# Channel fold by reflection: GpSimd forms the sums and differences of mirrored channels ahead of the fold's matmuls

## The chip, the cores and the metric

The kernel runs on all 8 cores of one Trainium2 chip. Each core computes one of the 8 sequences of the batch, and every core does the same work on its own data with its own copy of the weights. The metric is the device time of the slowest core in microseconds (us). The engines are called PE (TensorE), DVE (VectorE), ACT (ScalarE), POOL (GpSimd) and SP (SyncE, which only issues transfers here). POOL also issues transfers, and those of its transfers that read float32 and write bf16 convert on the way; they are called casts below where they go from memory to memory.

## The reference

Two layers, each with a norm, a token mixer, a gate and a residual. The change lies in the first layer's mixer, a two-dimensional Fourier transform over the 4096 positions and over the 256 channels of each of 8 groups, of which the real part is kept:

```python
def fourier_mixer(h, w_in, w_out):
    b, s, _ = h.shape
    proj = h @ w_in                                  # (s, 1024) @ (1024, 4096)
    xin, z = proj[..., :D_INNER], proj[..., D_INNER:]
    xg = xin.reshape(b, s, N_GROUPS, GROUP_DIM).astype(jnp.float32)   # 8 groups of 256
    y = jnp.fft.fft2(xg, axes=(1, 3), norm="ortho").real
    y = y.astype(h.dtype).reshape(b, s, D_INNER)
    return (y * jax.nn.silu(z)) @ w_out
```

The second layer is a gated mixer over chunks of 128 positions (`sgu_mixer`); the change does not touch it.

## The kernel before

The transform over channels is not applied to the 4096 rows of activations but to the weights: for each group g, `fold(g)` multiplies the 256 rows of the branch weight (bf16, two tiles `wb` of 128 channels x 1024) with a table `fmat` of 256 channels x 256 columns: 128 cosines and 128 sines, with the cosine of harmonic 128 in the place of the sine of harmonic 0. The result `wp[g % 2]` (1024 x 256, bf16) is then the weight of the group.

The layer runs through these stages, one after the other on PE:

- The first loop, over 32 tiles `s` of 128 rows: load (`load_x`, SP), square (ACT), `norm` (two small POOL instructions, then DVE), eight transposes into `hT` (PE, DVE), a first transform step `U` (PE), which is stored to `Ud` (SP), and in between gate projections `zgroup(hb, zt)`: eight matmuls of 512 columns, a SiLU by ACT into the tile `sz[zt % 6]`. `zt` is one of 16 blocks of gate channels with its weight `wz[zt % 6]`; `hb` is one of 8 blocks of 512 rows.
- The position transform, `qd` from 7 down to 0: PE reads `V` (loaded from `Ud` by 32 transfers on SP) and writes `H` through ACT and DVE. `fold(0)` is spread over qd 4 to 1.
- The group loop, g from 0 to 7: `pq(g)` (128 matmuls of 260 columns on `H` and `wp[g % 2]`, then DVE forms sum and difference), `gate(g)` (DVE multiplies the result into `sz[2g % 6]` and `sz[(2g+1) % 6]`, and puts a store of each of these two tiles to `gyT` on a list), then `fold(g+1)`, then the gate projections `zall(zt)` of two further blocks: 6, 7 after pq(1), 8, 9 after pq(2), 10, 11 after pq(3), 12 to 15 after pq(4). The block zt writes the tile that block zt - 6 had, so its first SiLU waits until that tile's store to `gyT` has landed.
- The passage to the second half: the stored `gyT` is read back as `gyt`, and the output projection `out0` starts.

Four things order the work around the change. Each engine, and each queue of transfers, works through its instructions in program order; a wait holds up all that stands behind it. `tick()` is called after each `qd` of `pq` and each `zgroup` of `zall`; every fourth call issues one cast of the later layers' weights (32 casts of 512 KB written, on POOL, `precasts`), and every fourth call also takes one store off the list (SP). A cast waits for the eighth one before it (`d_pc[n % 8]`). And PSUM has six float32 banks in turn (`next_f`), so PE can be six banks ahead of ACT.

Before, `wb` is loaded by POOL with conversion, two tiles per group, into slots of which two lie under `wp[1]` and four under `V`. The lines of the profile that matter are L431 (the fold's matmuls), L269 (its copy to `wp`), L412 and L416 (matmul and SiLU of a `zgroup`), L595 (`pq`), L626 (the gate's multiplies), L399 and L401 (the norm's POOL instructions), L166 (every transfer) and L114 (every wait of a queue).

## Time and profile before

| | us |
|---|---|
| median of three runs | 1583.35 |
| lowest of them | 1580.53 |
| the profiled execution | 1582.04 |
| its span on the slowest core, core 1 | 1580.7 |
| spans of all eight cores | 1564.3 to 1580.7 |

| engine, core 1 | busy us | share |
|---|---|---|
| PE | 1545.7 | 98% |
| DVE | 747.1 | 47% |
| ACT | 515.9 | 33% |
| POOL | 156.4 | 10% |

The profile follows one execution on its slowest core. Times of rows are microseconds from the start of the span; the span leaves 1.3 us of that execution's own time outside. A busy PE is not a PE at its peak, since matmuls overlap; the spacing of their starts is what one costs in a sequence.

### The profile page before, as it was taken

Reading aid. Unit: us, or ns where it says so; the run is one execution under the profiler, and the core shown is the slowest. Engines: PE = TensorE matmul, PEld = TensorE weight load, DVE = VectorE, ACT = ScalarE, POOL = GpSimd, SP = SyncE. Lnnn points to the kernel's source line nnn. Section 1 sums busy time; section 2 is a strip of 40 time slices with the busy share of each in tenths; the row PEclk is TensorE's granted clock in tenths of the full one; section 3 lists DMA queues with packets and bytes.
Section 4 is the critical chain, followed back from the end, with each engine's and each line's share of the span. In section 5 each row is a group of like instructions: output and inputs, shape, how many; then the busy total and the mean of one; then the engine's idle time right before and its main releaser. Section 6 shows DMA issues by size and latency. Waiting matters only on the chain.

```text
span 1580.7 us, 25439 instructions; the slowest of 8 cores (1564.3 to 1580.7 us)
## 1 busy us (share of the span) xinstructions
PE 1545.7 (98%) x8458; PEld 782.7 (50%) x8458; DVE 747.1 (47%) x1245; ACT 515.9 (33%) x915; POOL 156.4 (10%) x336
## 2 busy tenths in 40 slices
PE   6999999999899999999999999999999999999997
PEld 3557766646644444544444444445444444544443
DVE  5866532213636435624553463356245435624552
ACT  5766333333223313322331232133123313322331
POOL 3311111010211011001000100110010011001000
PEclk9999999999999999999999999999999999999999
DMA  9986999999887941643453155335324531643411
GB/s 256 288 249 170 171 139 152 152 144 180 250 205 189 242 176 48 226 150 98 152 199 125 38 188 199 107 116 201 134 69 167 207 113 47 226 152 96 148 46 54
DMA packets 103298, 247.72 MB, mean 157 GB/s; under 512 B 40042, under 2 KB 56042, under 8 KB 87402
## 3 DMA queue, kind: packets, MB, share of 16 engines
q1 hardware_dynamic: 53652, 207.76, 39.8%
q0 software_dynamic: 15568, 29.63, 14.9%
q10 hardware_dynamic: 33952, 8.72, 3.3%
q8 instruction: 71, 1.16, 0.3%
q14 instruction: 55, 0.45, 0.1%
HBM read 225.24 MB, written 58.87 MB: 180 GB/s over the span
## 4 chain that ended last, share of the span: by engine, by line
PE 94%; DMA 4%; DVE 1%; issue 1%; ACT 0%; SPq 0%; POOL 0%; DVEq 0%; ACTq 0%; POOLq 0%
PE pf L848 28%; PE pf L751 27%; PE pf L412 14%; PE pf L821 14%; PE pf L595 5%; PE pf L858 2%; DMA gy<-sz_77 1%; DMA a0x_59<-xt 1%; DMA gyt<-gy 1%; PE pb L481 1%; PE pf L491 1%; PE pf L558 1%; DMA h1T<-xn_0_2525 1%; PE pf L431 1%; SPq L166 0%
## 5 line engine op out<-in xcount | busy, mean ns | idle before, releaser
L751 PE MATMUL pf<-W_2513,gyt 128*128 128x512 bf16 x992 | 219.2, 382 | 7.4 <-DMA gyt<-gy 7.4
L751 PE MATMUL pf<-W_2524,u 128*128 128x512 bf16 x1024 | 222.3, 379 | 0.0
L751 PEld LDWEIGHTS pf<-W_2513,gyt 128*128 128x128 bf16 x992 | 97.6, 98 | 126.6 <-issue 13.0
L751 PEld LDWEIGHTS pf<-W_2524,u 128*128 128x128 bf16 x1024 | 100.2, 98 | 120.8
L851 ACT ACTIVATE u<-pf 128x512 bf16<-128x512 f32 x128 | 76.5, 597 | 164.2 <-PE pf L848 154.7
L825 ACT ACTIVATE v<-pf 128x512 f32<-128x512 f32 x128 | 75.4, 597 | 121.1 <-PE pf L821 101.6
L848 PE MATMUL pf<-h1T,ring_2522 128*128 128x512 bf16 x416 | 96.8, 385 | 0.0
L848 PE MATMUL pf<-h1T,ring_2519 128*128 128x512 bf16 x416 | 96.5, 382 | 0.0
L848 PE MATMUL pf<-h1T,ring_2523 128*128 128x512 bf16 x416 | 95.5, 380 | 0.0
L848 PE MATMUL pf<-h1T,ring_2520 128*128 128x512 bf16 x416 | 94.9, 379 | 0.0
L848 PE MATMUL pf<-h1T,ring_2521 128*128 128x512 bf16 x384 | 88.3, 379 | 0.0
L605 DVE TENSOR_TENSOR Dt_93<-pc_97,pf 128x256 bf16<-128x256 f32 x28 | 11.8, 421 | 144.9 <-PE pf L595 120.8
L862 DVE SCALAR_TENSOR_TENSOR ytmp_2532<-pf,gTs,TT 128x512 f32<-128x512 f32 x64 | 48.1, 751 | 48.6 <-PE pf L858 48.5
L742 POOL TENSOR_SCALAR sm_2546<-sm_2546 128x1 f32<-128x1 f32 x24 | 5.3, 221 | 631.6 <-ACT sqj L787 588.0
L848 PEld LDWEIGHTS pf<-h1T,ring_2522 128*128 128x128 bf16 x416 | 40.1, 99 | 44.4 <-issue 5.2
L848 PEld LDWEIGHTS pf<-h1T,ring_2523 128*128 128x128 bf16 x416 | 39.8, 98 | 43.8 <-issue 1.5
L848 PEld LDWEIGHTS pf<-h1T,ring_2519 128*128 128x128 bf16 x416 | 39.8, 98 | 43.6 <-issue 3.5
L848 PEld LDWEIGHTS pf<-h1T,ring_2520 128*128 128x128 bf16 x416 | 39.6, 98 | 43.3 <-issue 0.3
L851 ACT ACTIVATE sg_2543<-pf 128x512 bf16<-128x512 f32 x64 | 38.2, 598 | 69.2 <-PE pf L848 58.9
L851 ACT ACTIVATE sg_2544<-pf 128x512 bf16<-128x512 f32 x64 | 38.2, 598 | 67.6 <-PE pf L848 64.4
L595 PE MATMUL pf<-H,wp_85 128*128 128x260 bf16 x512 | 58.3, 276 | 0.0
L595 PE MATMUL pf<-H,wp_84 128*128 128x260 bf16 x512 | 57.6, 274 | 0.0
(298 smaller groups left out, 2317.8 us busy)
## 6 DMA issues: line engine op xcount, KB each, us to landing
ring_2519<-wind SPq DMA_DIRECT2D x20, 1024.0 KB, 7.4
ring_2520<-wind SPq DMA_DIRECT2D x19, 1024.0 KB, 7.1
ring_2521<-wind SPq DMA_DIRECT2D x19, 1024.0 KB, 6.7
ring_2522<-wind SPq DMA_DIRECT2D x19, 1024.0 KB, 7.1
ring_2523<-wind SPq DMA_DIRECT2D x19, 1024.0 KB, 6.4
gyt<-gy SPq DMA_DIRECT2D x7, 2048.0 KB, 12.4
wind<-w_in1p POOLq DMA_DIRECT2D x24, 512.0 KB, 42.1
V<-ud SPq DMA_DIRECT2D x32, 256.0 KB, 7.9
```

Source lines behind the costliest of these rows:

```text
L412: pe.op(lambda e: e.matmul(bank[:], w[:, dc, :], hT[:, dc, hb * 512:(hb + 1) * 512], start=(dc == 0), stop=(dc == 7)), [wb_, hTb[hb], hTal ...
L431: pe.op(lambda e: e.matmul(bank[:, h * 256:(h + 1) * 256], wb[wb_slot(2 * g + kc)][0][:, dc * 128:(dc + 1) * 128], fmat[:, kc, :], start=( ...
L481: pe.op(lambda e: e.transpose(out=bank[:, dc * 128:(dc + 1) * 128], in_=xn_[:, dc * 128:(dc + 1) * 128], identity=ident[:]), [xnb, identb] ...
L491: pe.op(lambda e: e.matmul(bank[:], tr[:], xn_[:, h * 512:(h + 1) * 512], start=True, stop=True), [trb, xnb], [bb], waw=False)
L595: pe.op(lambda e: e.matmul(bank[:, 0:HQ], w_[:, dc, cs * 128:(cs + 1) * 128], H[:, qd, dc, cs, :], start=(dc == 0), stop=(dc == 7)), [wpb, ...
L751: pe.op(lambda e: e.matmul(bank[:], lhs(kc), rhs[:, kc, nh * 512:(nh + 1) * 512], start=(kc == 0), stop=(kc == 15)), lb(kc) + rb(kc), [bb] ...
L821: pe.op(lambda e: e.matmul(bank[:], h1T[:, dc, t * 128:(t + 1) * 128], r_[:, dc, :], start=(dc == 0), stop=(dc == 7)), [h1Tb[t], rb], [bb] ...
L825: act.op(lambda e: e.activation(out=vj, in_=bank[:], func=AF.Gelu_apprx_tanh), [bb], [vjb])
L848: pe.op(lambda e: e.matmul(bank[:], r_[:, dc, c0:c0 + 128], h1T[:, dc, :], start=(dc == 0), stop=(dc == 7)), h1Tb + [rb], [bb], waw=False, ...
L851: act.op(lambda e: e.activation(out=out_ap, in_=bank[:], func=func), [bb], wb_)
L858: pe.op(lambda e: e.matmul(bank[:, t * 128:(t + 1) * 128], vhat[t][0][:, ct * 128:(ct + 1) * 128], wsT[:, ct // 2, :], start=True, stop=True),
L862: dve.op(lambda e: e.scalar_tensor_tensor(out=y_[:].rearrange("c (t p) -> c t p", p=128), in0=bank[:].rearrange("c (t p) -> c t p", p=128) ...
```

## The change

The cosines of channel c and channel 256 - c are equal, and their sines are opposite. So the fold needs only the sum of the two channels' weights for the cosines and the difference for the sines: 128 channels instead of 256 in each.

- The weights come as `wbE`, pairs of channels (c, 256 - c) in float32, in eight groups of four quarters of 256 columns. SP loads one quarter (128 x 2 x 256 float32, 256 KB) into a single staging tile `st`, and two POOL instructions write its sum and its difference as bf16 into `eo[:, 0]` and `eo[:, 1]`. `sums()` is a generator that does this in program order: one call issues the load, the next the two POOL instructions. Channels 0 and 128 make up the first pair; the even harmonics take its sum and the odd ones its difference, and so the harmonics are sorted even first (`_HARM`).
- `fold` takes one matmul of 129 columns on the sums and one of 192 on the differences in place of two of 256.
- The calls: one per tile in tiles 10 to 17 of the first loop (group 0), two after each of qd 7 to 4 (group 1), then one per `tick` (group 2 in pq(0), group 3 in pq(1), group 4 in zall(6); from group 4 on a group starts only when the fold two groups before it has been issued, so groups 5, 6, 7 come in zall(8), zall(10), zall(12)). `fold(g)` first issues what is missing.
- `eo` has four places: under `wp[1]`, under `wz[0]` and `wz[1]`, and two under `V`. As group 1 lies on `wz[0]` and `wz[1]`, the loads of the gate weights 6 and 7 move from the end of the position transform to after fold(1).
- The loads of `wb` on POOL are gone.

```diff
-            wb = [tile(f"wb{i}", [128, D], BF16, ...) for i in range(6)]
+            eo = [tile(f"eo{i}", [128, 2, D], BF16, o) for i, o in enumerate((top["at"] - 4096, wzo, vh, vh + 4096))]
...
+            st, stb = tile("st", [128, 2, 256], F32, top["at"] - 2048)
...
-            def load_wb(i):
-                k = wb_slot(i)
-                pool.dma(wb[k][0][:], wb_in[i], d_wb[k], writes=[wb[k][1]])
+            def eo_of(g):
+                return eo[g if g < 2 else 2 + g % 2]
+
+            folded = {"n": 0, "summed": 0}
+
+            def sums():
+                for g in range(8):
+                    eo_, eob = eo_of(g)
+                    while g > 3 and folded["n"] < g - 1:
+                        yield
+                    for q in range(4):
+                        sp.dma(st[:], wb_in[g, q], d_st, writes=[stb], waw=True)
+                        yield
+                        for k, op in enumerate((ALU.add, ALU.subtract)):
+                            pool.op(lambda e: e.tensor_tensor(out=eo_[:, k, q * 256:(q + 1) * 256], in0=st[:, 0, :],
+                                                              in1=st[:, 1, :], op=op), [stb], [eob], waw=False)
+                        folded["summed"] += 1
+                        yield
...
             def fold(g, dcs):
+                while folded["summed"] < 4 * g + 4:
+                    next(summing)
...
-                        for kc in range(2):
-                            pe.op(lambda e: e.matmul(bank[:, h * 256:(h + 1) * 256],
-                                                     wb[...][0][:, dc * 128:(dc + 1) * 128], fmat[:, kc, :],
+                        for k, f, a, z in ((0, fE, 0, 129), (1, fO, 64, 256)):
+                            pe.op(lambda e: e.matmul(bank[:, h * 256 + a:h * 256 + z], eo_[:, k, dc * 128:(dc + 1) * 128], f,
+                                                     start=(k == 0), stop=True, skip_group_check=(k == 1)),
...
-                    if 0 < g < 6:
-                        load_wb(2 * g + 4)
-                        load_wb(2 * g + 5)
+                    folded["n"] = g + 1
...
-                if s in (12, 14):
-                    load_wb(s // 2 - 6)
+                if 10 <= s < 18:
+                    next(summing)
...
                 if ticks["n"] % 4 == 1:
                     next(casts, None)
+                next(summing, None)
                 if stores and ticks["n"] % 4 == 0:
                     stores.pop(0)()
...
+                if folded["summed"] < 8:
+                    next(summing)
+                    next(summing)
                 if qd == 0:
-                    load_wb(2)
-                    load_wb(3)
-                    for i in range(6, 9):
-                        load_wz(i)
-                    load_wb(4)
-                    load_wb(5)
-                    for i in range(9, 11):
+                    for i in range(8, 11):
                         load_wz(i)
...
                     fold(1, range(4))
                     for hb in range(6, 8):
                         zgroup(hb, 5)
-                    load_wz(11)
+                    for i in (6, 7, 11):
+                        load_wz(i)
```

## Rows read from the trace of the kernel before

**Rows 1.** The page's chain that ended last: shares by engine and by line.

```profile
PE 94%; DMA 4%; DVE 1%; issue 1%; ACT 0%; SPq 0%; POOL 0%; DVEq 0%; ACTq 0%; POOLq 0%
```

**Rows 2.** Waits of PE: who was waited for, total us, times, longest.

```profile
PE pf L751 <- DMA gyt<-gy: 7.4, 1, 7.4
```

**Rows 3.** Chain at the passage, in order of time: start, us, what.

```profile
387.37 0.42 DVE Dt_93 L605
...
394.63 18.68 DMA gy<-sz_77
...
428.92 14.62 PE pf L751 x58
```

**Rows 4.** Chain in the group loop, a fold and a pq: start, us, what.

```profile
164.94 1.75 PE pf L431 x16
...
214.77 14.19 PE pf L595 x128
```

**Rows 5.** Timeline of PE, qd 4: start, us, instruction.

```profile
130.89 1.06 PE L558 MATMUL pf<-bdt,V 128*128 128x128 bf16 x16
131.78 0.27 PE L431 MATMUL pf<-cpk,wb_86 128*128 128x256 bf16 x1
```

**Rows 6.** POOL's groups by form: count, busy us, mean ns, idle before.

```profile
L626 POOL TENSOR_TENSOR szsp<-p_100,szsp 8x224 bf16<-8x224 f32 x1 | 0.6, 614 | 0.1
L626 POOL TENSOR_TENSOR szsp<-p_100,szsp 8x32 bf16<-8x32 f32 x1 | 0.3, 330 | 0.1
```

**Rows 7.** Timeline of POOL in the first loop: start, us, instruction, idle before.

```profile
59.57 0.22 POOL L399 TENSOR_SCALAR stats<-stats 128x1 f32<-128x1 f32 x1 [1.60 <-ACT a0xn_61 L391]
```

**Rows 8.** Timeline of SP's queue: start, us to issue, transfer.

```profile
107.51 20.81 SPq L166 DMA_DIRECT2D V<-ud  x32
169.25 0.33 SPq L166 DMA_DIRECT2D gy<-sz_72  x1
172.35 0.33 SPq L166 DMA_DIRECT2D gy<-sz_73  x1
...
381.20 0.34 SPq L166 DMA_DIRECT2D szsp<-zrow  x1
```

**Rows 9.** Transfers by line, several stretches: count, KB each, us to landing.

```profile
V<-ud SPq DMA_DIRECT2D x32, 256.0 KB, 7.9
out<-x_1_2516 SPq DMA_DIRECT2D x1, 256.0 KB, 2.1
gy<-sz_72 SPq DMA_DIRECT2D x1, 1024.0 KB, 16.7
gy<-sz_73 SPq DMA_DIRECT2D x1, 1024.0 KB, 20.0
gy<-sz_76 SPq DMA_DIRECT2D x1, 1024.0 KB, 13.0
wb_88<-wbT POOLq DMA_DIRECT2D x1, 256.0 KB, 5.4
zrow<-sz_75 ACTq DMA_DIRECT2D x3, 8.0 KB
```

**Rows 10.** Timeline of ACT, gate blocks 15 and 6: start, us, instruction.

```profile
373.85 0.20 ACTq L166 DMA_DIRECT2D zrow<-sz_75  x1
...
189.02 0.60 ACT L416 ACTIVATE sz_72<-pf 128x512 bf16<-128x512 f32 x1 [0.36 <-PE pf L412]
```

**Rows 11.** Timeline of PE, gate blocks 6 and 7.

```profile
186.98 13.98 PE L412 MATMUL pf<-hT,wz_78 128*128 128x512 bf16 x64
200.79 13.98 PE L412 MATMUL pf<-hT,wz_79 128*128 128x512 bf16 x64
```

**Rows 12.** One stretch: busy us of PE, PEld, DVE, ACT, POOL; clock, DMA share, GB/s.

```profile
187.00:215.00 28.00, 28.00 (x134) 12.84 (x132) 5.06 (x8) 10.57 (x21) 4.44 (x7) 1.00 1.04 180
```

**Rows 13.** Stretches around PE's wait at the passage, same columns.

```profile
427.00:429.00 2.00, 0.08 (x1) 0.11 (x2) 1.69 (x4) 0.00 (x0) 0.00 (x0) 0.50 0.97 314
431.00:433.00 2.00, 2.00 (x7) 0.78 (x6) 0.00 (x0) 0.00 (x0) 0.00 (x0) 0.59 0.90 287
```

47 lines of the change are left out of this document (25 added, 22 removed).

## The prediction

> **What bounds the kernel now.** I read the chain that ended last first: PE holds 94% of it [rows 1], so only what shortens or stalls PE's sequence moves the end. The waits of PE come next. In the whole group loop there is no wait worth the name; the one large wait is 7.4 us at the passage to the output projection, for the read-back of `gy` [rows 2]. Then the chain around that passage, in order of time: it leaves PE at the end of pq(5), goes over DVE's gate from 387.4, then over the store of `sz_77` issued at 394.6 and the read-back, and returns to PE at 428.9 [rows 3]. So PE time saved before 387 reaches the end; PE time saved between 387 and 421 only lengthens the 7.4 us wait. Last the stretches: from 187 to 215, gate blocks 6 and 7, the transfer engines are full (share 1.04) while they move only 180 GB/s [rows 12]; the casts fill them. The reader should keep that in mind: the change touches PE a little and the queues a lot.
>
> **The fold's matmuls.** Sixteen matmuls of 256 columns take 1.75 us, 109.4 ns each [rows 4]. Sixteen of 128 columns with a new weight each start at 130.89 and the next instruction at 131.78, so 55.6 ns each [rows 5]. Between the two points a column costs 0.42 ns: 129 columns 56 ns, 192 columns 82.5 ns. A pair falls from 218.8 to 138.5 ns, 80 ns saved; 8 pairs per fold save 0.64 us, 8 folds 5.1 us. Folds 6 and 7 lie behind pq(5), in the stretch that only feeds the 7.4 us wait. Folds 0 to 5 count: **-3.85 us**. The bounds are 0 (weight loads or ACT's copies set the pace) and -5.1.
>
> The Trainium skill speaks against part of this: TensorE: Matmul & The Clock Gate, section Back-to-back issue gap, gives about 81 ns for a sustained weight load and matmul of 128 columns and 131 ns for 512. An estimate from that page puts the pair at about 170 ns, the saving at 0.39 us a fold, and the sum 1.5 us later. This case's trace disagrees at 128 columns, with 55.6 ns [rows 5], and the row decides.
>
> **The sums on POOL.** No row has 128x256 float32. The nearest two-input row is 8x224 with 614 ns, and 8x32 took 330 ns: 1.48 ns an element, so 0.66 us at 256 and 1.3 us for the pair [rows 6]. Bounds: 0.66 (the two overlap entirely) and 2 us. In all 32 pairs, 42 us of an engine that is 10% busy. In the first loop a pair stands between two norms, where POOL idles 1.60 us per tile [rows 7]; 1.3 us fit, so I take 0, with a bound of 4 pairs x (2.0 - 1.6) = 1.6 us lost.
>
> **The loads, moved from POOL's queue to SP's.** There is one staging tile, so a quarter is a cycle: transfer, pair of sums, next transfer. Alone, 256 KB landed 2.1 us after its issue [rows 9]; with the sums I take a cycle of 4.1 us (transfer 2.8). Among the casts no load of this size was on SP. The lower bound is that same 2.1 us, the upper 13.0 us, the quickest gate store of 1 MB [rows 9]. The nearest row is an 8 KB transfer issued by ACT at 373.85, for which SP waited until 381.20: 7.4 us for hardly any data [rows 8 to 10]. Two gate stores issued 3.1 us apart landed after 16.7 and 20.0 us, so the second came 6.4 us behind the first [rows 8, 9]; a quarter of that would put 256 KB at 9.0. I take 8.5 us, and 9.8 us for a cycle. The bytes read are the same as before, and the `wb` loads' share of the queue is given back, so I price the total traffic at 0; its bound is 5 us either way at the passage, where the casts' end decides how long the 8 KB transfer takes.
>
> **Where this meets the path.** SP works in order. A store of a gate tile now stands behind a quarter whose transfer may not be issued before the last pair of sums, and POOL's casts and `wz` loads stand behind the sums. I follow the order through groups 1 to 4.
>
> - Group 1: the 32 V transfers are issued by 128.3, the last lands 7.9 us later [rows 8, 9], at 136. With nothing else moving, four cycles of 4.1 end at about 150.5. POOL then issues wz 8 to 10 and three casts.
> - Group 2: the first quarter lands before the casts fill the engines, sums done at 155.3. Three cycles of 9.8 would give 184.7; the casts issued by then run out towards 178, so I take 182. Only now come the loads of wz 6 and 7. The quickest load of that kind landed in 5.4 us [rows 9]: 188. PE reaches gate block 6 at 186.98 less three folds, 185.1 [rows 11]. **Stall 3 us** (0 to 6).
> - Group 3: after three `wz` loads and a cast, the first pair is done at about 190. Behind it SP issues the store of `sz_72`, at 190.4 where it was 169.25 [rows 8]. With the quickest 13 us [rows 9] it lands at 203. The first SiLU of block 6 writes that tile; before, it ran at 189.02, 3 us after the store had landed (169.25 + 16.7) [rows 8 to 10]. Six banks of 1.73 us (13.81 us for eight [rows 11]) let PE go on from 188 to 198.4. **Stall 5 us** (2 to 7).
> - The store of `sz_73` comes after the third quarter, which itself queues behind the store of `sz_72`: issued at about 206 where it was 172.35, landed at 218. Block 7 starts on PE at 207 and can run to 217.4. **Stall 1.5 us** (0 to 6).
> - Group 4: `sz_74` and `sz_75` land at about 235 and 250; blocks 8 and 9 start at about 237 and 251 and have 10.4 us of banks: none. Groups 5 to 7 begin one per 43 us of PE and a group takes some 35 us: none.
>
> The sum of the stalls is **+9.5 us**, between 4 and 15. A pause of PE has a further price: at the passage, where PE had paused for 7.4 us [rows 2], the granted clock was 0.50, the lower level of 1.2 GHz, at 427 to 429 and still 0.59 on average in 431 to 433, when PE worked again [rows 13]. Some 4 us at half speed lose 2 us; for a pause of 5 us I take that as the upper bound and leave it in the range. Against the execution's own time: 1582.0 - 3.85 + 9.5 = 1587.7, so **1588**; the median of the three runs shown is 1.3 us above that execution.
>
> **Rivals.**
>
> - **The waits stay hidden; the saving alone.** If a quarter among the casts takes 4 us rather than 8.5, group 2 ends at about 169, wz 6 is there in time, the store of `sz_72` leaves at 175 and that of `sz_73` at 194, and the six banks cover both. For it speaks that POOL, held by the sums, has fewer casts in flight than before; against it the 7.4 us for 8 KB [rows 8 to 10]. 1582.0 - 3.85 = 1578, or 1582 if the shorter matmuls save nothing.
> - **The cycle is longer, 10 to 12 us.** Then wz 6 lands at 191 or later, the stalls are about 6, 8 and 5, fold(2) waits for its sums as well, and the clock falls in each pause: 1600 (1598 to 1615).
> - **The slower side: the cycle passes PE's period.** PE spends about 43.6 us on a group: pq 14.2 and fold 1.75 [rows 4], two gate blocks 27.6 (13.81 each [rows 11]). With two stores queued between, a group of four quarters takes 2 x 9.8 + 2 x 14.3 = 48 us if each store holds its quarter for its full 13 us. Should that hold in every group, the lag is carried on: the store of `sz_74` in block 12 leaves some 25 us after block 14 wants the tile, and folds 6 and 7 wait too. It decides from 43.6 us a group on, that is from a cycle of about 8 us beside fully serial stores. Price 30 to 45 us: 1612 to 1625. Against it speaks that a POOL that waits issues no casts, so that the queue drains and the cycle shortens by itself.
> - **Faster by over 2%** would need 32 us. All folds together are 8 x 1.75 = 14 us, and the passage holds 7.4 more; I see no way.
>
> **How the numbers follow.** Forecast (1588, its own range 1580 to 1598) 0.46; saving alone 0.30; longer cycle 0.13; the carried lag 0.09; faster by over 2% 0.02. The range from 1574 to 1606 holds the first two cases, the first with the passage's 5 us either way, and more than half of the third. Two per cent, 32 us, is about what a measurement of this kernel can tell from no change. Within it lie the first three cases, 0.89; slower 0.09; faster 0.02.
>
> **What would show it.** In the profile after: `fold` at about 1.1 us where it was 1.75; POOL pairs of 1.3 us, no norm in the first loop delayed by more than 1 us; quarters that land in 2 to 3 us before 150 and in 8 to 9 after; PE waits at blocks 6 and 7, the first on the load of wz 6, the next through ACT's SiLU on the stores of `sz_72` and `sz_73`, 4 to 15 us in all; stores at about 190 and 206. If PE has no wait between 180 and 220, the saving-alone case holds. If PE waits again in block 9 or later, or a fold waits on sums after group 3, it is the carried lag. A stall in the first loop would be something that I have priced at nothing.

## The result, and the profile after

| | before | after |
|---|---|---|
| executions without a disturbance, us | 1580.53, 1583.08, 1583.35 | 1591.96, 1592.44 |
| ratio after to before, 95% interval | | 1.0062 [1.0033, 1.0092] |
| span of the slowest core in the profiled execution, us | 1580.7 (core 1) | 1590.6 (core 4) |

The changed kernel is 9.9 us later, 0.6%. Two of its four executions were disturbed on one die (1654.83 and 1881.68) and are left out, as is one of the kernel before. The page and the rows below are of core 4. In the changed kernel L454 is the fold, L432 and L436 the matmul and the SiLU of a `zgroup`, L614 is `pq`, L770 `out0`, L399 the sums, L419 and L421 the norm on POOL, L172 every transfer.

The chain that ended last, shares by engine, now holds a term that it did not have [rows 1]: PE's part fell from 94% to 89%, and transfers rose from 4% to 7%. A line further down on the page gives the quarters `st<-wbE` 3% of the span.

```profile
PE 89%; DMA 7%; POOL 1%; DVE 1%; issue 1%; ACT 0%; DVEq 0%; ACTq 0%; POOLq 0%; SPq 0%
```

Waits of PE (engine, line, releaser: us in all, times, longest). The first answers to [rows 2]. The `a0xn_60` one is the start of the program and was 8.2 us before as well (core 6).

```profile
PE pf L770 <- DMA gyt<-gy: 9.2, 1, 9.2
PE pb L502 <- DVE a0xn_60 L423: 8.1, 1, 8.1
PE pb L502 <- DVE hT L505: 5.4, 4, 2.9
PE pf L454 <- POOL eo_88 L399: 4.9, 1, 4.9
PE pf L432 <- DMA wz_78<-wz: 3.8, 1, 3.8
```

PE's timeline around the first of the moved loads (start, us, instructions, idle before and its releaser). It answers to [rows 11]: block 6 started at 186.98 and took 13.98 us; it now starts at 198.90 and takes 16.51, and the fold before it waits too.

```profile
192.77 2.30 PE L454 MATMUL pf<-cpk,eo_88 128*128 128x129 bf16 x16 [4.93 <-POOL eo_88 L399]
198.90 16.51 PE L432 MATMUL pf<-hT,wz_78 128*128 128x512 bf16 x64 [3.83 <-DMA wz_78<-wz]
215.24 7.07 PE L432 MATMUL pf<-hT,wz_79 128*128 128x512 bf16 x32
```

The stretches of that place (busy us of PE, PEld, DVE, ACT, POOL; granted clock, DMA share, GB/s), the third as in [rows 12]. The clock falls to the lower level of 1.2 GHz once PE has paused, is still there in 199 to 201, when PE works without a gap, and is back at 2.4 GHz in 205 to 207. The transfer engines, full in this stretch before (1.04), are at 0.73, and at 0.22 in 150 to 160 (0.90 before, on core 1).

```profile
193.00:196.00 3.00, 2.07 (x16) 1.69 (x13) 2.46 (x4) 2.35 (x5) 1.82 (x4) 0.50 0.31 81
199.00:201.00 2.00, 2.00 (x6) 0.63 (x6) 0.00 (x0) 0.00 (x0) 0.00 (x0) 0.50 1.03 83
187.00:215.00 28.00, 19.25 (x87) 9.29 (x86) 7.27 (x13) 6.60 (x14) 9.77 (x15) 0.76 0.73 143
150.00:160.00 10.00, 8.84 (x82) 6.91 (x82) 4.99 (x16) 5.16 (x14) 4.63 (x8) 1.00 0.22 55
205.00:207.00 2.00, 2.00 (x11) 0.88 (x9) 0.00 (x0) 0.00 (x0) 0.00 (x0) 1.00 1.06 356
```

The chain of waits through group 2, and a later fold. Load, sums, load, sums: one staging tile, and quarters that land in 10 us. The fold of 1.13 us answers to the 1.75 of [rows 4].

```profile
163.97 10.12 DMA st<-wbE
...
174.22 2.31 POOL eo_88 L399 x2
...
176.59 9.80 DMA st<-wbE
...
192.46 6.03 DMA wz_78<-wz
...
243.41 1.13 PE pf L454 x16
```

The two gate stores on SP's queue, where [rows 8] has 169.25 and 172.35, and the SiLUs of ACT that wait for them.

```profile
198.95 0.63 SPq L172 DMA_DIRECT2D gy<-sz_72  x1
...
214.31 1.08 SPq L172 DMA_DIRECT2D gy<-sz_73  x1
```

```profile
210.96 3.54 ACT L436 ACTIVATE sz_72<-pf 128x512 bf16<-128x512 f32 x7 [14.54 <-DMA gy<-sz_72]
...
221.06 1.08 ACT L436 ACTIVATE sz_73<-pf 128x512 bf16<-128x512 f32 x2 [4.96 <-DMA gy<-sz_73]
```

POOL's timeline, first at the end of group 0 in the first loop, then at groups 6 and 7. Three things are to be seen. At 72.89 a pair waits 3.31 us for its quarter, and the norm of a tile stands behind it. From 326 to 372 POOL mostly waits for quarters, as long as 10.84 us for one. And the casts, which one tick in four should issue one by one, go out five and six together as soon as a group's last pair is done; the last six, and the load of `wsT` that stands behind all casts, leave at 368 to 372. In the kernel before, POOL ran ahead and issued `wsT` at 345.0 on the slowest core.

```profile
64.13 1.86 POOL L399 TENSOR_TENSOR eo_86<-st 128x256 bf16<-128x256 f32 x2
...
72.89 1.41 POOL L399 TENSOR_TENSOR eo_86<-st 128x256 bf16<-128x256 f32 x2 [3.31 <-DMA st<-wbE]
74.39 0.22 POOL L419 TENSOR_SCALAR stats<-stats 128x1 f32<-128x1 f32 x1
...
327.41 3.41 POOL L172 DMA_DIRECT2D wind<-w_in1p  x5
332.83 1.49 POOL L399 TENSOR_TENSOR eo_89<-st 128x256 bf16<-128x256 f32 x2 [2.02 <-DMA st<-wbE]
345.15 1.41 POOL L399 TENSOR_TENSOR eo_89<-st 128x256 bf16<-128x256 f32 x2 [10.84 <-DMA st<-wbE]
...
357.47 1.40 POOL L399 TENSOR_TENSOR eo_89<-st 128x256 bf16<-128x256 f32 x2 [10.25 <-DMA st<-wbE]
367.00 1.41 POOL L399 TENSOR_TENSOR eo_89<-st 128x256 bf16<-128x256 f32 x2 [8.14 <-DMA st<-wbE]
368.36 4.07 POOL L172 DMA_DIRECT2D wind<-w_in1p  x6
372.40 0.59 POOL L172 DMA_DIRECT2D wsT<-w_sT  x1
```

The wait at 72.89 reaches PE. DVE's scaling behind that norm waits 3.32 us, then PE's transposes wait 2.93, and the eight matmuls of a `zgroup` behind them take 2.92 us where the eight just before the pause took 1.89. The last of these rows is the stretch in which that happens, with a granted clock of 0.53, mostly the lower level of 1.2 GHz. On core 4 this is nearly all of the 4.8 us that the first loop loses: 2.93 of waiting, and some 1.6 at the lower clock (an estimate: 3.40 us at 0.53).

```profile
77.59 0.87 PE L502 MATMUL pb<-ident,a0xn_61 128*128 128x128 bf16 x8 [2.93 <-DVE hT L505]
...
79.11 2.92 PE L432 MATMUL pf<-hT,wz_78 128*128 128x512 bf16 x8
...
77.60:81.00 3.40, 3.40 (x15) 1.72 (x16) 3.40 (x5) 0.60 (x1) 0.22 (x1) 0.53 1.00 200
```

The same comparison by stage, from the starts on PE's timelines of every core in the two profiled executions (range over the eight cores, us):

| stage | before | after |
|---|---|---|
| end of the first loop | 99.2 to 101.8 | 104.1 to 109.0 |
| pq(0) to pq(1), one fold | 19.4 to 19.6 | 18.8 |
| pq(1) to pq(2), one fold, blocks 6 and 7 | 43.6 to 44.6 | 47.4 to 55.6 |
| pq(2) to pq(3), one fold, blocks 8 and 9 | 43.6 | 42.9 |
| pq(4) to pq(5), one fold, blocks 12 to 15 | 71.2 | 70.6 |
| start of `out0` | 419.8 to 428.9 | 432.4 to 443.2 |
| start of `out0` to the end | 1144 to 1154 | 1145 to 1148 |

Core 4 of both: the first loop gives +4.8, five folds give -0.64 each, pq(1) to pq(2) gives +12.7 beside its fold's -0.64, and pq(7) to `out0` +0.9; `out0` starts 15.1 us later. From the slowest core of before to the slowest of after it starts 14.3 us later (428.9 on core 1, 443.2 on core 4). Nearly all of that is PE's lateness at the end of pq(5): the chain at the passage begins on DVE at 399.96 where it began at 387.37 [rows 3], 12.6 us later, and from there to `out0` it takes 43.2 us where it took 41.6.

```profile
399.96 0.42 DVE Dt_91 L624
...
407.22 20.87 DMA gy<-sz_77
...
431.73 11.09 DMA gyt<-gy
...
443.17 14.28 PE pf L770 x58
```

Of the 14.3 us only 9.9 arrive, since core 1 before took 1151.8 us from `out0` to the end and core 4 after takes 1147.4. The rows for this lie in the kernel before. Behind the passage its core 1 has five stretches, 27.5 us in all, with a granted clock of 0.81, between the two levels of 1.2 and 2.4 GHz, while PE is busy throughout; two of them are shown. They cost some 5.2 us (an estimate: 0.19 of 27.5). Cores 0, 2 and 3 have such stretches too; cores 4 to 7 have none, and no core of the changed kernel has any.

```profile
442.80:449.00 6.20, 6.20 (x25) 2.61 (x24) 2.10 (x3) 1.15 (x2) 0.79 (x2) 0.81 0.97 383
...
955.30:961.90 6.60, 6.60 (x27) 2.72 (x25) 2.00 (x5) 1.79 (x3) 0.00 (x0) 0.81 0.76 286
```

Among cores 4 to 7 alone the slowest takes 1574.6 us before (core 6) and 1590.6 after, 16.0 us or 1.0% more. So 9.9 us is what was measured, and the change by itself probably costs more. Whether the timed executions of the kernel before had such stretches is not on record.

### The profile page after: what moved, and what is told of

Same layout as the page of the kernel before. It is cut to its first block, busy times and chain, and to the rows that moved or that the text cites. A ratio compares the mean times of both kernels' runs of the same rounds, so it can differ in the third digit from the quotient of the medians.

```text
span 1590.6 us, 25582 instructions; the slowest of 8 cores (1578.3 to 1590.6 us)
## 1 busy us (share of the span) xinstructions
PE 1539.8 (97%) x8458; PEld 779.0 (49%) x8458; DVE 750.2 (47%) x1245; ACT 514.6 (32%) x915; POOL 195.9 (12%) x384
## 3 DMA queue, kind: packets, MB, share of 16 engines
q0 software_dynamic: 13264, 25.43, 12.6%
## 4 chain that ended last, share of the span: by engine, by line
PE 89%; DMA 7%; POOL 1%; DVE 1%; issue 1%; ACT 0%; DVEq 0%; ACTq 0%; POOLq 0%; SPq 0%
PE pf L867 28%; PE pf L770 27%; PE pf L840 14%; PE pf L432 13%; PE pf L614 4%; DMA st<-wbE 3%; PE pf L877 2%; DMA gy<-sz_77 1%; DMA a0x_54<-xt 1%; DMA gyt<-gy 1%; PE pb L502 1%; DMA h1T<-xn_0_2559 1%; PE pf L512 1%; PE pf L580 0%; DMA wz_78<-wz 0%
## 5 line engine op out<-in xcount | busy, mean ns | idle before, releaser
L770 PE MATMUL pf<-W_2547,gyt 128*128 128x512 bf16 x992 | 218.1, 381 | 9.2 <-DMA gyt<-gy 9.2
L770 PE MATMUL pf<-W_2558,u 128*128 128x512 bf16 x1024 | 222.3, 379 | 0.0
L770 PEld LDWEIGHTS pf<-W_2547,gyt 128*128 128x128 bf16 x992 | 97.3, 98 | 127.5 <-issue 11.6
L770 PEld LDWEIGHTS pf<-W_2558,u 128*128 128x128 bf16 x1024 | 100.2, 98 | 120.8
L881 DVE SCALAR_TENSOR_TENSOR ytmp_2566<-pf,gTs,TT 128x512 f32<-128x512 f32 x64 | 48.1, 751 | 48.8 <-PE pf L877 48.5
L867 PEld LDWEIGHTS pf<-h1T,ring_2556 128*128 128x128 bf16 x416 | 39.7, 98 | 43.2
L867 PEld LDWEIGHTS pf<-h1T,ring_2554 128*128 128x128 bf16 x416 | 39.6, 98 | 43.2
L614 PE MATMUL pf<-H,wp_84 128*128 128x260 bf16 x512 | 57.6, 274 | 1.0 <-ACT wp_84 L462 1.0
L614 PE MATMUL pf<-H,wp_85 128*128 128x260 bf16 x512 | 57.4, 274 | 0.0
```

The costliest lines, as they stand in the source:

```text
L614: pe.op(lambda e: e.matmul(bank[:, 0:HQ], w_[:, dc, cs * 128:(cs + 1) * 128], H[:, qd, dc, cs, :], start=(dc == 0), stop=(dc == 7)), [wpb, ...
L770: pe.op(lambda e: e.matmul(bank[:], lhs(kc), rhs[:, kc, nh * 512:(nh + 1) * 512], start=(kc == 0), stop=(kc == 15)), lb(kc) + rb(kc), [bb] ...
L867: pe.op(lambda e: e.matmul(bank[:], r_[:, dc, c0:c0 + 128], h1T[:, dc, :], start=(dc == 0), stop=(dc == 7)), h1Tb + [rb], [bb], waw=False, ...
L881: dve.op(lambda e: e.scalar_tensor_tensor(out=y_[:].rearrange("c (t p) -> c t p", p=128), in0=bank[:].rearrange("c (t p) -> c t p", p=128) ...
```

## The experiments

Each ratio is to runs of the kernel before on the same chip. The three groups of four kernels ran on three chips; on these the kernel before had medians of 1575.34, 1574.12 and 1574.15 us. The changed kernel itself did not run beside these runs. Its 1.0062 (1.0033 to 1.0092) comes from executions beside which the kernel before took some 8 us longer than it takes here, so the ratios below can't be set against it closely. Run 12, less the 3.2 us that five shorter folds save, gives an estimate of 1.0075 for it on the third chip, if that saving reaches the end.

**1. The short matmuls alone.**

The base is the kernel before.

```diff
-                        for kc in range(2):
-                            pe.op(lambda e: e.matmul(bank[:, h * 256:(h + 1) * 256],
-                                                     wb[wb_slot(2 * g + kc)][0][:, dc * 128:(dc + 1) * 128], fmat[:, kc, :],
+                        for kc, a, z in ((0, 0, 129), (1, 64, 256)):
+                            pe.op(lambda e: e.matmul(bank[:, h * 256 + a:h * 256 + z],
+                                                     wb[wb_slot(2 * g + kc)][0][:, dc * 128:(dc + 1) * 128], fmat[:, kc, a:z],
```

> The kernel before, loads and all, but the fold takes one matmul of 129 and one of 192 columns from its two weight tiles in place of two of 256. It leaves out part of the fold's sum, so only its time is of use. It measures the saving alone. By spacings of rows of before (55.6 ns at 128 columns, 109.4 at 256): a fold of 1.11 us where it was 1.75, 0.64 us saved per fold, 3.85 us on the path; ratio to before 0.9976. By the page TensorE: Matmul & The Clock Gate of the Trainium skill, section Back-to-back issue gap (81 ns at 128 columns), an estimate of 0.39 us a fold and 0.9985. If ACT's copies set the pace of a fold, nothing: 1.000.

Measured: 1.0013 [1.0003, 1.0022]. Every fold is 0.64 us shorter: pq(1) to pq(2) takes 42.9 us on all eight cores. The gain is nevertheless gone at the end. Four cores (1, 2, 4, 6) end after 1557.0 to 1563.5 us, the other four after 1569.9 to 1573.3; the first start `out0` at 413 to 418, the second at 424 to 427. On core 5, a late one, PE waits for the read-back longer than in [rows 2]; core 1, an early one, has no such wait:

```profile
PE pf L751 <- DMA gyt<-gy: 11.6, 1, 11.6
```

So the first term of the prediction is right on PE and is given back at the passage, on the cores that end last. I took from this a second theory: from 150 on the transfer engines are a bound of their own. The rows of the kernel before fit it; in every stretch of 10 us from 160 to 370 and on every core the DMA share is 0.93 or more.

**2. Group 0's sums later in the first loop.** The base of this run and of the next four is the changed kernel.

```diff
-                if 10 <= s < 18:
+                if 22 <= s < 30:
                     next(summing)
```

> The changed kernel, with group 0's loads and sums in tiles 22 to 29 of the first loop, where no more x tiles are loaded, in place of tiles 10 to 17. First theory: the first loop lost its 3 to 8 us because a pair of sums waited on POOL for its quarter behind x tiles on SP's queue, with the next norm behind it. Then the loop ends at 99 to 102 us on every core as before (it ended at 104 to 109), and the time falls by 3 to 6 us, ratio to before about 1.003. Rival: the pairs of sums themselves, 1.9 us each between norms that leave 1.6 us, cost it: 4 x 0.3 us and no more is recovered by moving them, the loop ends at 104 or later, ratio unchanged at 1.006.

Measured: 1.0074 [1.0061, 1.0087]. The loop ends at 102.4 to 106.7: little is won. A pair takes less there (1.43 where it was 1.86), but waits for its quarter as before, on core 2 of this run:

```profile
87.44 1.43 POOL L399 TENSOR_TENSOR eo<-st 128x256 bf16<-128x256 f32 x2 [2.08 <-DMA st<-wbE]
...
94.70 1.42 POOL L399 TENSOR_TENSOR eo<-st 128x256 bf16<-128x256 f32 x2 [3.40 <-DMA st<-wbE]
```

**3. Three staging tiles for group 2** (two in the place of group 3's sums, which is free then).

```diff
+            st_ab = [tile(f"st_ab{i}", [128, 2, 256], F32, vh + 4096 + 2048 * i) for i in range(2)]
...
+                    if g == 2:
+                        places = [(st, stb), st_ab[0], st_ab[1], (st, stb)]
...
+                        for q in range(3):
+                            load(q)
+                        yield
+                        for q in range(4):
+                            sum_quarter(g, q, *places[q])
+                            if q == 0:
+                                load(3)
+                            yield
```

> The changed kernel, with three staging tiles for group 2 (two of them in the place that group 3's sums get later), so that three quarters are issued before the casts pile up. First theory, the serial cycle through one staging tile: group 2's sums end at about 168 in place of 192, fold(2) waits for nothing (it waited 4.9 us on core 4), PE's wait for the weight of block 6 goes (3.8 us), the store of sz_72 leaves at 176 to 180 in place of 199; from pq(1) to pq(2) PE takes 44 to 46 us where it took 47 to 56; the time falls by 4 to 8 us, ratio about 1.002. Rival: the transfer engines are simply full from 160 on, and the order of the quarters makes no difference: pq(1) to pq(2) stays above 47 us, ratio 1.006.

Measured: 1.0066 [1.0053, 1.0080]. fold(2) no longer waits, and pq(1) to pq(2) takes 42.9 to 49.0 us where it took 47.4 to 55.6. What is left there, on core 1, is the load of wz 6 behind the sums (3.4 us), and the store of `sz_72`, still at 191.39 behind a quarter of group 3. The serial cycle was thus one cause of the wait. `out0` starts at 418.3 to 432.3, 11 to 14 us before that of the changed kernel; how much of this arrives at the end the ratio can't tell, since the changed kernel did not run beside it.

**4. Runs 2 and 3 together, and group 3's sums not before block 6,** so that both gate stores go first.

```diff
-                next(summing, None)
+                if not 8 < ticks["n"] <= 16:
+                    next(summing, None)
```

> Both of these, and group 3's sums moved from pq(1) to gate block 6 (group 4's to block 7), so that the stores of sz_72 and sz_73 are not behind quarters in SP's queue. If the three losses (first loop, group 2's cycle, late stores) are all that the change adds, what is left is the saving of the shorter matmuls: no wait of PE over 1 us between the first loop and the passage, ratio 0.997 to 1.000. Rival: the stores come late again one pair of blocks further on, since group 3 and 4 now stand there: PE waits in blocks 8 and 9, ratio 1.001 to 1.005.

Measured: 1.0090 [1.0074, 1.0105], above both expectations, and later than run 3 on the same chip. On core 6 the stores leave from 173.45 on, close to [rows 8], and no SiLU waits for them; but the load of wz 6, issued at 176.5 with 2 MB of stores and seven casts around it, lands when PE has waited 14.4 us. pq(1) to pq(2) takes 49.4 to 60.2.

```profile
PE pf L459 <- DMA wz<-wz: 14.4, 1, 14.4
```

**5. No casts beside the quarters of groups 2 and 3.**

```diff
-                if ticks["n"] % 4 == 1:
+                if ticks["n"] > 16 and ticks["n"] % 4 == 1:
+                    next(casts, None)
+                if 16 < ticks["n"] <= 40 and ticks["n"] % 4 == 3:
                     next(casts, None)
...
-                    for _ in range(2):
-                        next(casts, None)
```

> The changed kernel without any cast before the 17th tick (pq(0) and pq(1) run without them); from there two per four ticks until the 40th, so that from the 40th tick on as many are issued as before. Theory (the quarters are late because they share the transfer engines with the casts, and the stores behind them are late for that): a quarter lands in 3 to 4 us, group 2 is summed by 165, wz 6 is loaded by 175, the stretch from pq(1) to pq(2) is 43 us on every core where it was 47 to 56, and the ratio is 1.000 to 1.003 (the first loop's 3 to 8 us stay). Rival (one staging tile and the order of the queues suffice for the stalls, whatever else is in flight): 48 to 55 us and 1.005 to 1.007.

Measured: 1.0153 [1.0137, 1.0169]. Both halves of this are of use. The theory's first half holds exactly: pq(1) to pq(2) is 42.9 to 43.0 us on all eight cores, every stall is gone. The ratio lies some 13 us above the higher of the two expectations. The time comes back later: pq(4) to pq(5) takes 75 to 83 us instead of 70.6, and `out0` starts at 440.7 to 452.7. On core 6 the transfer engines were half idle from 150 to 200 (0.51) and full afterwards:

```profile
150.00:200.00 50.00, 49.76 (x376) 35.97 (x377) 29.50 (x84) 18.08 (x41) 19.48 (x26) 0.97 0.51 122
...
300.00:380.00 80.00, 70.87 (x395) 38.20 (x394) 13.43 (x40) 21.24 (x43) 20.35 (x28) 0.97 0.96 157
```

and the gate stores of blocks 12 to 15 land late behind the casts that were put off (ACT waits 32.5 us for three of them between 300 and 385).

**6. Group 0 through four staging tiles** in the place of `sz5`, which the first loop does not use; `first_load(q)` loads quarter q into tile q, `first_sum(q)` issues its pair.

```diff
-                if 10 <= s < 18:
-                    next(summing)
+                if 8 <= s < 12:
+                    first_load(s - 8)
+                if s in (14, 17, 20, 23):
+                    first_sum((s - 14) // 3)
```

> The changed kernel with group 0 through four staging tiles of its own, in the place of sz5, which the first loop does not use: the loads are issued in tiles 8 to 11, the sums in tiles 14, 17, 20 and 23, so POOL never waits for a quarter there. Theory (the first loop loses its time because POOL waits for a late quarter and the norm stands behind it): the loop ends at 100 to 102 where it ended at 104 to 109, ratio 1.003 to 1.005. Rival (the pair of sums itself, 1.9 us there, delays the norm): the loop ends at 103 to 106 as in the run with the sums in tiles 22 to 29, ratio 1.006 to 1.007.

Measured: 1.0056 [1.0038, 1.0074]. The loop ends at 99.8 to 102.4, as in the kernel before. The pair still takes 1.86 us, but no longer waits:

```profile
59.98 1.86 POOL L411 TENSOR_TENSOR eo<-st 128x256 bf16<-128x256 f32 x2
...
69.99 1.86 POOL L411 TENSOR_TENSOR eo<-st 128x256 bf16<-128x256 f32 x2
```

This settles the first loop: it was the wait for a late quarter, with the norm behind it, and not the sums. The ratio lies 0.0019 below the estimate for the changed kernel, with an interval that reaches 0.0018 to either side.

**7. Denser casts from the 33rd tick on,** in the kernel of run 1.

```diff
-                if ticks["n"] % 4 == 1:
+                if (ticks["n"] % 4 if ticks["n"] <= 32 else ticks["n"] % 3) == 1:
```

> The kernel before with the short matmuls on the old tiles (the fold leaves out a part of its sum), as in the first of these runs, and from the 33rd tick on a cast every third tick in place of every fourth, so that the last is issued at about 325 where it was 370. Theory (the 3.85 us of the fold are given back at the passage, since the casts and the loads behind them fill the transfer engines from 300 to 410 at a rate of their own): the passage from pq(7) to the output projection takes 27 to 29 us on all cores where it took 27 to 38, and the ratio is 0.994 to 0.998. Rival 1 (the bytes of the passage alone set its end): unchanged, 1.000 to 1.002. Rival 2 (denser casts delay the gate stores of blocks 8 to 13): PE waits between 230 and 330, above 1.003.

Measured: 1.0020 [1.0009, 1.0032]. The edit did not do what it was for: `wsT`, behind the last cast, is issued at 336 to 352 as in run 1 (326 to 352). POOL waits 93.8 us for earlier casts, since a cast waits for the eighth before it. The casts go at the pace of the transfer engines, not of the ticks. It tells nothing more of the passage.

**8. Group 0 as in run 6, no cast before the 17th tick, then one every second tick.**

```diff
-                if ticks["n"] % 4 == 1:
+                if ticks["n"] > 16 and ticks["n"] % 2 == 1:
```

> The changed kernel with both: group 0 through the four staging tiles, and no cast before the 17th tick, from there one every second tick (the last is issued at about 290). If the losses are the late quarter in the first loop, the casts beside the quarters of groups 2 and 3, and the casts at the passage, the ratio is 0.994 to 0.999. If any of the three is something else, its size stays: 1.002 to 1.006. If the denser casts delay the stores of blocks 8 to 12, PE waits between 200 and 290 and the ratio is above 1.003 too.

Measured: 1.0210 [1.0156, 1.0264], from executions of 1602.3, 1602.4 and 1616.3 us. The first loop (100.0 to 101.6) and pq(1) to pq(2) (42.9) are whole, and pq(4) to pq(5) takes 105 to 110 us: the last named case, at a later place than named. On core 1, between 300 and 400, ACT's waits are

```profile
ACT sz L447 <- DMA gy<-sz: 54.9, 3, 22.5
```

Runs 5 and 8 have this in common: from 150 to 200 the transfer engines are about half used (0.51, and 0.55 on core 1 of run 8), and the casts that were put off go out more densely afterwards, beside the gate stores of blocks 12 to 15, which come late. Whether the unused time or the denser casts make the stores late these two runs do not part.

**9. The kernel before, with two casts moved into the gap of its transfers.** `pool.deps([Vb[0]], [])` lets POOL wait until the last V transfer has landed.

```diff
+            pool.deps([Vb[0]], [])
+            for _ in range(2):
+                next(casts)
             act.load = dve.load = 0.0
             for qd in range(7, -1, -1):
```

> The kernel before, whole, with one thing moved: its first two casts are issued as soon as the last V transfer has landed (about 137), in the stretch to 150 in which the transfer engines of the kernel before are empty; the others keep their ticks, so that each of them comes eight ticks, some 14 us, earlier. Theory (from 150 to 400 the transfer engines are a second bound beside PE, full in every stretch of 10 us, and their end sets the passage): about 13 us of transfer work move ahead, the loads behind the casts end earlier, the store of sz_77 lands in 12 to 15 us where it took 18.7, and PE's wait of 7.4 for the read-back shrinks to 0 to 3: ratio 0.994 to 0.998. Rival (what is transferred beside the passage does not set its end; PE and the gate do): 0.999 to 1.001.

Measured: 0.9987 [0.9978, 0.9997], 1572.1 us beside 1574.15. The gap was there (DMA share 0.01 from 137 to 150 before on core 1, 0.58 here on core 0), and PE's wait at the passage falls as expected, on core 6 to

```profile
PE pf L754 <- DMA gyt<-gy: 1.9, 1, 1.9
```

`out0` starts at 416.6 to 421.6 on all cores. The time falls by 2 us only, where 3 to 9 were expected. The interval reaches the theory's range at one end and the rival's (0.999 to 1.001) at the other, so it is the shorter wait, and not the time, that speaks for the theory. The spans still differ by 9 us from core to core (1560.3 to 1569.2), though `out0` starts within 5. On the slowest, core 0, PE waits once more behind the passage, for the load of `h1T`, and the granted clock is 0.50 from 452.6 to 456.0; core 1, which is early, has neither this wait nor one at the passage.

```profile
PE pf L824 <- DMA h1T<-xn: 2.9, 1, 2.9
```

This is the fastest whole kernel of the study, faster than both kernels of the case.

**10. The same two casts, with the short matmuls** (the edits of runs 1 and 9).

> The same two early casts in the kernel with the short matmuls on the old tiles (the fold leaves out a part of its sum). That kernel without the early casts had 1.0013: its 3.85 us were given back at the passage. Theory of the full transfer engines: with their work moved ahead the saving arrives, 0.0015 to 0.0025 below the run with the early casts alone: 0.992 to 0.996. Rival (the saving is lost in another place, or the passage is bound by PE and the gate): no lower than the run beside it, 0.998 to 1.001.

Measured: 0.9973 [0.9961, 0.9985]. That lies between the two ranges. Without the early casts these matmuls had 1.0013 [1.0003, 1.0022]: the interval is clear of it. The intervals of this run and of run 9 overlap, but both ran on the same chip, so that their times can be compared directly: five executions of 1568.8 to 1570.8 us here, ten of 1570.4 to 1573.6 us there, and the means differ by 2.3 us. That is some two thirds of what five folds save (3.2 us): most of the saving arrives once the transfers leave room for it.

**11. Other places and another order in the changed kernel.**

```diff
-                return eo[g if g < 2 else 2 + g % 2]
+                return eo[0 if g == 0 else 3 - g % 2]
...
+                    while g > 2 and ticks["n"] < 16:
+                        yield
...
-                    for i in range(8, 11):
+                    for i in range(6, 11):
                         load_wz(i)
```

> The changed kernel with other places and another order, and the same arithmetic: group 0 through the four staging tiles in the place of sz5; group 1's sums lie under V (as those of groups 3, 5, 7), through three staging tiles of which two lie where group 2's sums go, so that wz 6 and 7 are free and are loaded where they were before; group 3's sums start at the 17th tick, behind the stores of sz_72 and sz_73. Theory (the 4 to 13 us of the group loop are the displaced loads of wz 6 and 7 and the stores behind quarters): the first loop ends at 100 to 102, pq(1) to pq(2) takes 43 to 47, ratio 1.000 to 1.003. Rival (any sum that stands beside the casts holds the queues, wherever it lies): 48 or more there, or as much lost later, ratio 1.005 to 1.008.

Measured: 1.0119 [1.0100, 1.0138]. The first loop ends at 99.3 to 102.5 and pq(1) to pq(2) takes 42.9 to 48.2, at most 44.3 on seven cores: the theory of the stalls holds. But the ratio lies above both expectations. A part is lost before pq(0), which starts 50.5 to 54.3 us after the end of the first loop, where it was 48.8 in the kernel before; the larger part is lost at the passage. PE's wait there on core 3, the slowest:

```profile
PE pf L808 <- DMA gyt<-gy: 16.9, 1, 16.9
```

On this core pq(5) starts at 377.1, 8.4 us before core 4 of the changed kernel, and `out0` at 442.5, only 0.7 us before it. POOL's timeline ends alike in both: the quarters of group 7 one by one, then six casts at once.

```profile
356.70 1.41 POOL L426 TENSOR_TENSOR eo<-st 128x256 bf16<-128x256 f32 x2 [9.29 <-DMA st<-wbE]
367.67 1.41 POOL L426 TENSOR_TENSOR eo<-st 128x256 bf16<-128x256 f32 x2 [9.56 <-DMA st<-wbE]
369.01 4.06 POOL L172 DMA_DIRECT2D wind<-w_in1p  x6
373.06 0.58 POOL L172 DMA_DIRECT2D wsT<-w_sT  x1
```

**12. The staging alone: the changed kernel with long matmuls.**

```diff
-                        for k, f, a, z in ((0, fE, 0, 129), (1, fO, 64, 256)):
+                        for k, f in ((0, cpk[:, 0:256]), (1, cpk[:, 130:386])):
```

> The changed kernel with its fold made long again: two matmuls of 256 columns on the staged sums (the columns are not the reference's, so the fold computes another transform). This is the staging alone, without the saving. If the saving of 0.64 us per fold reaches the end in the changed kernel, this run is later than the changed kernel by 2.5 to 4 us: 1.0080 to 1.0095. If the transfer engines set the end there too, as in the run with the short matmuls on the old tiles, it stays at 1.0055 to 1.0070.

Measured: 1.0095 [1.0081, 1.0110]. It lies in the range of the first case, and the changed kernel's 1.0062 below it; but that was not measured beside it, and its interval goes up to 1.0092. That the saving reaches the end in the changed kernel is likely by this and not shown.

**One view over all of them.** When POOL has issued its last cast it issues the load of `wsT`. From there to the first matmul of `out0`, over all eight cores of each profiled execution:

| kernel | `wsT` issued, us | `out0` starts, us | difference, us | start of pq(5) to `out0`, us |
|---|---|---|---|---|
| changed kernel | 362 to 372 | 432.4 to 443.2 | 68.1 to 72.9 | 53.3 to 57.7 |
| run 2 | 353 to 372 | 424.3 to 439.1 | 67.3 to 73.7 | 51.3 to 55.2 |
| run 3 | 348 to 364 | 418.3 to 432.3 | 68.0 to 72.4 | 48.4 to 56.1 |
| run 4 | 352 to 373 | 425.9 to 443.4 | 66.2 to 74.3 | 49.6 to 54.8 |
| run 5 | 373 to 379 | 440.7 to 452.7 | 67.2 to 73.7 | 63.3 to 68.8 |
| run 6 | 352 to 364 | 423.9 to 435.1 | 69.5 to 72.2 | 50.3 to 55.6 |
| run 11 | 352 to 373 | 422.7 to 442.5 | 66.8 to 74.7 | 54.7 to 66.1 |
| run 12 | 356 to 370 | 425.6 to 443.8 | 68.6 to 73.5 | 48.9 to 54.8 |
| kernel before | 335 to 355 | 419.8 to 428.9 | 73.4 to 85.2 | 49.9 to 57.5 |
| run 9 | 319 to 343 | 416.6 to 421.6 | 77.8 to 97.6 | 48.5 to 50.6 |
| run 1 | 326 to 352 | 413.3 to 427.2 | 73.7 to 87.4 | 48.4 to 60.1 |
| run 7 | 336 to 352 | 416.1 to 427.8 | 74.9 to 80.5 | 49.9 to 61.6 |
| run 10 | 317 to 341 | 413.5 to 418.4 | 76.6 to 97.4 | 48.3 to 51.2 |
| run 8 | 397 to 402 | 450.7 to 464.3 | 53.6 to 64.6 | 48.3 to 57.1 |

In the eight kernels with the sums on POOL and casts every fourth tick (run 5 for its first part apart), the difference is 66 to 75 us on all 64 cores. In run 8, with denser casts, it is smaller; where POOL has no sums to wait for, it is longer and not constant. That two times go together does not show that one sets the other: in six of the eight kernels (all but runs 5 and 11) `wsT` leaves 11 to 25 us before PE begins pq(5), and a core that is late in the one is late in the other.

The last column parts them. The shortest passage from pq(5) to `out0` in the table takes 48.3 us; what a core takes beyond that is mostly its wait for the read-back (9.2 of the 57.7 us on core 4 of the changed kernel; the 57.1 of run 8 are on its cores 0 and 1, where PE itself is slower). In the changed kernel the passage takes 53.3 to 57.7 us, not far from the 49.9 to 57.5 of the kernel before. So its loss against the kernel before is in the main PE's own lateness at pq(5), and the transfers add little more than they added before. In run 5 the passage takes 63.3 to 68.8 us. In run 11 it takes 54.7 and 56.3 on the two cores on which `wsT` leaves at 352, and 61.7 to 66.1 on the others, on which it leaves at 364 or later. There PE's stalls between pq(1) and pq(2) are gone or nearly so, and the late transfers set the start of `out0` instead.

So a third sequence runs close behind PE in the changed kernel: 24 quarters, one after the other, on one staging tile from 158 to 367, each a cycle of 5 to 6 us while single casts leave and of mostly 10 to 14 us behind a burst of casts, with the casts behind them. On core 4 POOL waits for nothing but quarters in that time. That `out0` goes with this sequence once PE's stalls are taken away is shown by runs 5 and 11. That a shorter sequence (casts on a queue that no sum holds up) would bring the end forward is argued from the table; no run did that alone.

## Why the prediction was right, and which terms were not

The forecast was 1588 with 1580 to 1598 as its own range; the measured time is 1592, 1.0062 times the kernel before. That the two lie so close is in part luck. The sum added 5.6 us to an execution of 1582.0 us whose slowest core had lost some 5 us behind the passage, at the granted clock of 0.81. The changed kernel lost nothing of that kind there, and its `out0` starts 14.3 us later, not 5.6. On core 4 the terms were short by 4.8 us in the first loop, 3.2 in the stalls, 0.6 in the folds and about 1 at the passage. Point by point:

- **The fold's matmuls.** A fold takes 1.13 us and was priced at 1.11. An estimate by the rule that was weighed against it (the Trainium skill, TensorE: Matmul & The Clock Gate, section Back-to-back issue gap) is 1.36; the row decided rightly. The sum was too large by one fold: the first loop's end to pq(0) takes 48.8 us before and after on core 4, so fold(0), spread over the position transform, saves nothing there. Five folds give 3.2 us and not 3.85. Where I erred more is in "PE time saved before 387 reaches the end". Run 1 shows that it did not, in the kernel before: the passage gave it back. The 7.4 us wait was on the table in [rows 2], and I had read it as slack behind 387 only, not as a sign that the transfers had an end of their own.
- **The sums.** 1.41 us a pair where the engines are quiet, 1.86 in the first loop, for the 1.3 taken; inside the bounds of 0.66 and 2.
- **The first loop, the mis-sized term.** Priced at 0 with a bound of 1.6 us, measured +3 to +8. I compared the pair's length with POOL's idle 1.60 us [rows 7] and asked only whether the sums fit. The step that failed is that I gave the quarter's landing no time there: a transfer issued beside the loads of `x` and the stores of `U` comes late, POOL waits in order, the norm behind it is late, then DVE's scaling, which waits 3.32 us, PE's transposes, which wait 2.93, and the matmuls behind them, at the lower clock. Run 6 takes that wait away, with pairs as long as before (1.86 us), and the loop is whole. The last sentence of the prediction named this place as one priced at nothing.
- **The stalls at blocks 6 and 7.** Forecast 9.5 us, 4 to 15; measured 4.5 to 12.7, on core 4 12.7. The size held and the parts did not. The cycle was 11.7 and 12.3 us where I took 9.8, which is the cycle of the rival named the longer cycle; group 2's sums ended at 192.5 and not at 182, and wz 6 landed at 198.5 and not at 188. On core 4 the stall is fold(2) on its sums (4.9 us, forecast 0), block 6 on wz 6 (3.8, forecast 3), and the lower clock after these pauses: block 6 took 16.51 us for 13.98 and the fold 2.30 for 1.13, together 3.7 us, where I had left up to 2 in the range. 4.9 + 3.8 + 3.7 is 12.4 of the 12.7. The stores of `sz_72` and `sz_73` left at 199 and 214, later than the 190 and 206 I had written, and ACT waited 14.5 and 5.0 us for them, but PE was late already and its six banks covered that: stalls that I had added up lay side by side. So the mechanism was that of the rival of the longer cycle. Its 1600 was too late against the measured 1592, because of this and because the 1582.0 that it started from held the 5 us at the clock of 0.81.
- **The later groups.** No wait of PE in blocks 8 to 15, as forecast, and 0.64 us gained in each. But "a group takes some 35 us: none" was too short a look. Groups 3 and 4 took POOL 26 and 22 us, but then the casts that had been held went out in bursts, and groups 5 to 7 took 41 to 44 us each behind them. I priced the traffic at 0 because the bytes were the same and left 5 us either way at the passage, "where the casts' end decides". What moved was not the bytes but the order: casts in program order behind sums that wait. `wsT`, behind the last cast, left at 362 to 372 where it had left at 335 to 355. On the slowest cores the passage grew by only 1.6 us (41.6 to 43.2), within those 5 us. The rival of the carried lag had looked for a lag in the gate's blocks; it sits in the casts.
- **What stays open.** How much each of the two sequences would cost alone: PE's sequence without POOL's late casts was never run. How late the changed kernel is against its own variants, since it did not run beside them. And why the two early casts of run 9 bring only 2 us; the wait of the kernel before at the passage on that chip is not on record.

## What to carry to other kernels

When work is moved to an engine that also issues transfers, its waits become the waits of everything that it issues behind them: follow not only who needs the result, but when the last transfer behind it leaves. Where the transfer engines read about 1.00 in every stretch, as in the kernel before from 160 to 370, treat them as a second bound: the time saved on PE showed up as a longer wait for the read-back (run 1), and most of it arrived once an empty stretch was filled first (run 10). A short load beside long queues was bought with several buffers issued far ahead (run 6), not with a later place for its consumer (run 2). And before two times are subtracted, compare the granted clock of the two executions stage by stage: here a lower clock in the kernel before hid a part of what the change cost.

## What the runs showed of the hardware that I had not expected

- A transfer of 256 KB on SP's queue landed 2.7 to 2.8 us after its issue when nothing else moved, and 8 to 12 us after it when casts had just been issued on POOL's queue (core 4 of the changed kernel); a cast of 512 KB landed 42.1 us after its issue in the kernel before (median) and 24.0 in the changed one. A new transfer does not stand behind all that is in flight, but it shares with it.
- With the casts of the kernel before the transfer engines read 0.97 to 1.16 at 96 to 226 GB/s (core 1, stretches of 10 us from 210 to 380); after the casts they read 1.00 at 288 GB/s (380 to 400). The profile lists a cast with the 512 KB that it writes and not with the float32 that it reads, so part of the difference may lie in the counting. The busy share of the transfer engines is no measure of the bytes listed.
- After pauses of 4.9 and 3.8 us, with PE at work between them, the granted clock was still 0.50 from 199 to 203 with PE busy throughout, and 1.00 from 205: the pause cost 3.7 us beyond its own length.
- On cores 0 to 3 of the kernel before the granted clock fell to 0.81 for 4 to 8 us at a time while PE was busy throughout; cores 4 to 7 of the same execution have no such stretch behind the passage.
